# Head norm through selectors into one bank, and products of constants at the borders of stages

## The reference, cut to what matters

```python
h = rms_norm_2(h_res, norm_gain[li]);  proj = h @ w_in[li]
f_in, q, k, v, gate = jnp.split(proj, splits, axis=-1)
f_out = fourier_mixer(f_in, w_fourier[li])
q = q.reshape(b, l, N_ATTN_HEADS, 2, HEAD_DIM)        # 4 x 2 heads of 64
k = k.reshape(b, l, N_ATTN_HEADS, 2, HEAD_DIM)
q = apply_partial_rotary(rms_norm_2(q, q_norm_gain[li]), cos, sin)
k = apply_partial_rotary(rms_norm_2(k, k_norm_gain[li]), cos, sin)
...
o = diff_attention(q, k, v, lam)
y = jnp.concatenate([f_out, a_out], axis=-1) * jax.nn.silu(gate)
h_res = h_res + y @ w_out[li]
```

## Time and profile before

| | |
|---|---|
| median of 3 runs | 2792.8 us (2792.77 to 2797.52) |
| the profiled execution's own time | 2796.85 us |
| its span in the trace | 2795.1 us |
| PE busy | 2642.2 us, 95% of the span, 14429 matmuls |
| DVE, ACT, POOL busy | 1434.5, 1054.1 and 456.4 us |
| mean granted clock of the TensorE | 0.972 |

### The profile page before, as it was taken

One profiled execution on the slowest core, in us unless ns is written; L12 is line 12 of the kernel. 1 busy time (PEld: TensorE's weight loads), 2 busy tenths in 40 slices (PEclk: granted clock), 3 DMA queues, 4 the chain that ended last, 5 costly groups with the idle time before them and its releaser, 6 DMA issues. The chain is left out here.

```text
span 2795.1 us, 35915 instructions
## 1 busy us (share of the span) xinstructions
PE 2642.2 (95%) x14429; PEld 2265.9 (81%) x14429; DVE 1434.5 (51%) x2019; ACT 1054.1 (38%) x1846; POOL 456.4 (16%) x283
## 2 busy tenths in 40 slices
PE   5999869899889999999999999989999999989999
PEld 1877766899777888888888999779989999768987
DVE  5743682333457666666658423347743522326751
ACT  3412443444245334333344222157722222227740
POOL 0002201332000000000000000048820000008940
PEclk8999979999989999999999999999999999999999
DMA  5531101000211112112111233232122113233222
GB/s 234 181 132 48 41 5 53 16 1 1 106 39 53 38 61 61 44 48 61 46 53 48 92 82 82 78 78 47 43 101 106 48 42 84 57 106 74 55 83 84
DMA packets 67570, 189.46 MB, mean 68 GB/s; under 512 B 8016, under 2 KB 26832, under 8 KB 66512
## 3 DMA queue, kind: packets, MB, share of 16 engines
q1 hardware_dynamic: 67408, 187.22, 21.9%
HBM read 146.79 MB, written 16.97 MB: 59 GB/s over the span
## 5 line engine op out<-in xcount | busy, mean ns | idle before, releaser
L2649 DVE SCALAR_TENSOR_TENSOR res<-ps,gates,res 128x1024 f32<-128x1024 f32 x120 | 148.6, 1279 | 100.0 <-PE ps L2773 100.0
L1285 PE MATMUL ps<-h_hi,pf_wh 128*128 128x346 f32 (+2 forms) x800 | 187.8, 338 | 0.3
L1285 PE MATMUL ps<-h_lo,pf_wh 128*128 128x346 f32 (+2 forms) x800 | 183.0, 333 | 0.0
L2508 ACT ACTIVATE wo_wh<-ff_raw 128x512 fp32r<-128x512 f32 x120 | 75.3, 628 | 280.3 <-DVE ff_raw L2619 114.2
L1921 DVE TENSOR_REDUCE da_negmax<-ps 128x1 f32<-128x1040 f32 x136 | 167.9, 1236 | 20.9 <-PE ps L1775 14.1
L1906 POOL TENSOR_TENSOR da_E<-da_E,da_F 128x1040 f32<-128x1040 f32 x68 | 164.6, 2421 | 5.7
L2773 PE MATMUL ps<-ff_h_hi,wo_wh 128*128 128x512 f32 x512 | 157.8, 389 | 1.4 <-DVE res L2649 1.3
L1818 PE MATMUL ps<-da_aT,v 128*128 128x128 f32 (+1 forms) x1224 | 158.1, 275 | 0.7 <-ACT qk L1878 0.7
L2773 PE MATMUL ps<-ff_h_lo,wo_wh 128*128 128x512 f32 x512 | 157.7, 389 | 0.0
L2773 PE MATMUL ps<-ff_h_hi,wo_wl 128*128 128x512 f32 x512 | 157.6, 389 | 0.0
L1292 PE MATMUL ps<-h_hi,pf_wl 128*128 128x346 f32 (+2 forms) x800 | 152.4, 338 | 0.0
(11 more groups left out here) (540 smaller groups left out, 6154.9 us busy)
## 6 DMA issues: line engine op xcount, KB each, us to landing
ff_raw<-w_ff SPq DMA_DIRECT2D x48, 512.0 KB, 3.5
ada_w<-w_ada SPq DMA_DIRECT2D x16, 1024.0 KB, 7.3
ff_raw<-w_in SPq DMA_DIRECT2D x20, 512.0 KB, 4.1
pf_raw<-w_in SPq DMA_DIRECT2D x20, 512.0 KB, 4.2
wo_raw<-w_out SPq DMA_DIRECT2D x18, 512.0 KB, 4.4
residual_spill<-res SPq DMA_DIRECT2D x16, 520.0 KB, 3.1
st_q<-st_q_rounded SPq DMA_DIRECT2D x32, 260.0 KB, 5.1
ada_w<-w_ada SPq DMA_DIRECT2D x4, 2048.0 KB, 16.8
```

The lines of the kernel that those rows point to most:

```text
L1285: pe.matmul(bank(i * 2 + s, s)[c], wh[:, s, q * P:(q + 1) * P], x(q)[:, a:a + ln], start=(q == 0 and n == 0), stop=False)
L2508: act.activation(ring(wh, i), src, ACT.Copy).then_inc(s_hi, 1)
L2649: last = dve.scalar_tensor_tensor(out=res[:, m, :], in0=k.ps[:, b:b + 2, :].rearrange("p c w -> p (c w)"), scalar=gate[:, m:m + 1], in1=re ...
```

## The change

It has two parts. The diff below is cut to its core.

**Head norm.** ACT squares tile n and then rounds the square (hi, line `s_hi`); DVE makes the rest (lo, `rests`). A selector `pick` of 128 partitions and mostly zeros is the stationary operand: a window of 128 columns of it has two columns with ones, at row `32 c + 2 n` and the next of the output. Six matmuls per tile n (hi and lo, three chunks) add the sums of both half heads and of chunk c into rows `32 c + 2 n` of one bank, all 48 into the same 348 columns. They stand at (m, 7), and for the odd n at (m + 1, 3), one tile later than before. DVE multiplies the 128 x 348 sums twice by the root R (copied to the same layout), ACT takes one root with scale and epsilon per partition, DVE the reciprocal, a product by R, ACT rounds, DVE takes the rest. There are no transposes. Each of the 24 pieces has its own 128 x 128 selector, made by POOL.

**Products of constants.** `busy(n)` issues n matmuls of the constant `ones` with the identity, 128 x 128 in float32, into a bank that is not in use; nobody reads them. A stage gets some before its first work (`before`) and some after its last one (`behind`, after the wait that frees the bank).

```diff
+def busy(pe, k, bank, n):
+    for _ in range(n):
+        pe.matmul(k.ps[:, bank, 0:P], k.ones[:], k.ident[:], start=True, stop=True)
 ...
+                busy(pe, k, idle_bank, before)
                 loop(pe, body)
+                if behind:
+                    pe.wait_ge(freed[0], NI)
+                    busy(pe, k, 0, behind)
 ...
-    SUMS = {(m, 3 + 4 * i): 2 * m + i for m in range(4) for i in range(2)}
-    TURNS = {(4, 4): 0, (4, 5): 1, (4, 7): 2}
+    SUMS = {(m, 7): 2 * m for m in range(4)} | {(m + 1, 3): 2 * m + 1 for m in range(4)}
     SPREAD = {(5 + u // 8, u % 8): u for u in range(24)}
 ...
-            pe.wait_ge(self.s_sq, n + 1)
-            for t in range(self.NT):
-                w = min(P, L2 - t * P)
-                mm = pe.matmul(k.ps[0:w, 6, 16 * t + 2 * n:16 * t + 2 * n + 2], self.sq[n % 2][:, t * P:t * P + w],
-                               k.half_ones[:, 0:P:64], start=True, stop=True)
+            pe.wait_ge(self.s_lo, n + 1)
+            for i, sq in enumerate((self.hi[n % 2], self.lo[n % 2])):
+                for c, (a, w) in enumerate(self.cx):
+                    first = self.ones_at - self.row(n, c)
+                    mm = pe.matmul(k.ps[:, 6, 0:w], self.pick[:, first:first + P], sq[:, a:a + w],
+                                   start=(n == 0 and i == 0 and c == 0), stop=(n == self.N - 1 and i == 1 and c == len(self.cx) - 1))
             mm.then_inc(self.s_ssq, 1)
 ...
-            pe.matmul(k.ps[:, 6 + u % 2, 0:w], row, self.rh[:, a:a + w], start=True, stop=False)
-            pe.matmul(k.ps[:, 6 + u % 2, 0:w], row, self.rl[:, a:a + w], start=False, stop=True).then_inc(self.s_sp, 1)
+            pe.matmul(k.ps[:, 6 + u % 2, 0:w], self.spread[u][:], self.rh[:, 0:w], start=True, stop=False)
+            pe.matmul(k.ps[:, 6 + u % 2, 0:w], self.spread[u][:], self.rl[:, 0:w], start=False, stop=True).then_inc(self.s_sp, 1)
 ...
                 if n >= 2:
                     act.wait_ge(self.s_ssq, n - 1)
-                act.activation(self.sq[n % 2][:], self.qk[:, n, :], ACT.Square).then_inc(self.s_sq, 1)
+                act.activation(sq, self.qk[:, n, :], ACT.Square).then_inc(self.s_sq, 1)
+                act.wait_ge(self.s_sq, n + 1)
+                act.activation(hi[:], sq, ACT.Copy).then_inc(self.s_hi, 1)
 ...
+    def rests(self, dve, m):
+        for n in (2 * m, 2 * m + 1):
+            dve.wait_ge(self.s_hi, n + 1)
+            dve.tensor_tensor(self.lo[n % 2][:], self.sq[n % 2][:], self.hi[n % 2][:].bitcast(F32), ALU.subtract).then_inc(self.s_lo, 1)
 ...
         if m == 4:
             dve.wait_ge(self.s_ssq, self.N)
+            dve.tensor_tensor(self.rs[:], k.ps[:, 6, 0:self.w], self.root[:], ALU.mult).then_inc(self.s_var, 1)
+            dve.wait_ge(self.s_var, 1)
+            dve.tensor_tensor(self.rs[:], self.rs[:], self.root[:], ALU.mult).then_inc(self.s_var, 1)
             dve.wait_ge(self.s_sd, 1)
+            dve.reciprocal(self.rs[:], self.rs[:]).then_inc(self.s_r, 1)
+            dve.wait_ge(self.s_r, 1)
+            dve.tensor_tensor(self.rs[:], self.rs[:], self.root[:], ALU.mult).then_inc(self.s_r, 1)
+            dve.wait_ge(self.s_rh, 1)
+            dve.tensor_tensor(self.rl[:], self.rs[:], self.rh[:].bitcast(F32), ALU.subtract).then_inc(self.s_rl, 1)
```

More of the change, by code:

```diff
@@ L1406, in _ @@
             def _(pe):
+                busy(pe, k, 7, before)
                 for g, ts in enumerate(groups):
@@ L1429, in _ @@
                     pe.sem_inc(summed, 1)
+                if behind:
+                    pe.wait_ge(out_lo if split else out_hi, 5)
+                    busy(pe, k, 4, behind)
             if side:
@@ L1842, in _ @@
                         scores(g, 1)
+                    if i < 0:
+                        busy(pe, k, 7, 6)
                     if 0 <= i < NG:
@@ L2288, in latent_attention @@
     at0 = h0 + 4 * 5152 + MH * LT * 4
-    gemm(nc, k, "uk", rows(d["w_uk"]), MH, 2, lambda q: kh[:, q, :], lambda q: kl[:, q, :], call, preloaded=True, norm=norm, then=("mv", lambda q: d["w_mv"][q % 2 * P:(q % 2 + 1) * P, :], MH * MV, 3), side=keys,
+    gemm(nc, k, "uk", rows(d["w_uk"]), MH, 2, lambda q: kh[:, q, :], lambda q: kl[:, q, :], call, preloaded=True, norm=norm, before=14, behind=4, then=("mv", lambda q: d["w_mv"][q % 2 * P:(q % 2 + 1) * P, :], MH * MV, 3), side=keys,
          evac_act=copy_out(lambda m, a, w: kraw[:, m, a:a + w] if isinstance(m, int) else kraw[:, bass.ds(m, 1), a:a + w], call))
@@ L2292, in latent_attention @@
                 lambda q, a: kh[:, q, a:a + P], lambda q, a: kl[:, q, a:a + P],
-                list(range(0, LT, P)), lambda t: (v[:, t, :],), preloaded=True, then=("uq", rows(d["w_uq"]), 3 * P, 2))
+                list(range(0, LT, P)), lambda t: (v[:, t, :],), preloaded=True, behind=4, then=("uq", rows(d["w_uq"]), 3 * P, 2))
     qpe = k.sb("q_pe", [P, MH, L], k.res0 - 512)
@@ L3627, in project @@
             silu(act, m - 12, s, i, banks, freed, first)
-    gemm(nc, k, f"pf{li}", rows(d["w_in2"], R0), 20, KD, XH, XL, cx, evac_act=project, evac_dve=times_root, preloaded=True, norm=norm, late=norm,
+    gemm(nc, k, f"pf{li}", rows(d["w_in2"], R0), 20, KD, XH, XL, cx, evac_act=project, evac_dve=times_root, preloaded=True, norm=norm, late=norm, before=7, behind=6,
          split_first=k.split[f"pf{li}"], chunks_at=lambda m: cg if isinstance(m, int) and m >= 12 else cx,
@@ L3637, in second_layer @@
                 lambda q, a: hh[:, q * L2 + a:q * L2 + a + P], lambda q, a: hl[:, q * L2 + a:q * L2 + a + P],
-                list(range(0, L2, P)), lambda t: (v[:, t, :],), preloaded=True, side=stacks, row_scale=norm.rc, also=last_silu)
+                list(range(0, L2, P)), lambda t: (v[:, t, :],), preloaded=True, side=stacks, row_scale=norm.rc, also=last_silu, before=2, behind=8)
     yb = qk
@@ L3660, in second_layer @@
         own = [k.sb(f"pf1_first_{part}", [P, KD * P], p0 + 4096 * x, F32R)[:] for x, part in enumerate(("hi", "lo"))]
-        more = dict(follow=follow, then=("pf1", rows(d["w_in2"], 20 * P), KD * P, 2), split_next={1: own}, stored=follow.s_kept,
+        more = dict(follow=follow, behind=5, then=("pf1", rows(d["w_in2"], 20 * P), KD * P, 2), split_next={1: own}, stored=follow.s_kept,
                     store_tile=lambda m: (spill[:, m:m + 1, :], k.res[:, m:m + 1, :]) if isinstance(m, int)
@@ L3712, in project @@
         last.then_inc(freed, 1)
-    gemm(nc, k, "ina", rows(d["w_ina"]), 8, KD, XH, XL, cx, norm=n1, preloaded=True, split_first=tuple(per_slot(t) for t in k.split["ina"]), then=("inb", rows(d["w_inb"]), KD * P, 2),
+    gemm(nc, k, "ina", rows(d["w_ina"]), 8, KD, XH, XL, cx, norm=n1, before=12, behind=4, preloaded=True, split_first=tuple(per_slot(t) for t in k.split["ina"]), then=("inb", rows(d["w_inb"]), KD * P, 2),
          evac_act=project,
@@ L3743, in first_block @@
                                 gain=lambda q: k.a1[:, 2, q:q + 1], shift=lambda q: k.mod[:, 24 + q, 0:1])], y0, F0 + 72 * L)
-    mix_out(nc, k, d["xT"], "wo1", rows(d["w_out"]), yh, yl, cx, k.gates[:, 0, :], L, norm=split, first_raw=k.raw["wo1"], preloaded=True, follow=n2, then=("ff", rows(d["w_ff"]), KD * P, 2), split_next={})
+    mix_out(nc, k, d["xT"], "wo1", rows(d["w_out"]), yh, yl, cx, k.gates[:, 0, :], L, norm=split, first_raw=k.raw["wo1"], preloaded=True, follow=n2, before=12, then=("ff", rows(d["w_ff"]), KD * P, 2), split_next={})
     n2.keep_tiles(k.sb("ffn_in_kept", [P, 4, 4, L // 2], F0 + 40 * L), fh, fl)
```

134 lines of the change are left out of this document (66 added, 68 removed).

## The result

The kernel after the change takes 2746.55 us (median of 4 runs, 2744.62 to 2751.60) beside 2793.58 us before (4 runs): a ratio of 0.983 [0.9815, 0.9849]. The measured time lies 5.6 us above the forecast of 2741 us and inside its range; 47.0 us were won where 51.5 were forecast. Between the two profiled executions it is 50.6 us (2796.85 to 2746.22, where 2745.3 was forecast for the latter).

A forecast was written before the change was run, and what follows sets the result against it. PE was taken as the bound, busy 2642 of 2795 us. From the profiled 2796.85 us, 31.4 for the head norm and 20.1 net for the clock gave 2745.3; less 4.05 to the median, 2741 us, range 2722 to 2766.

The forecast's parts named there:

- Head norm, removed and added: In pf0 and pf1: 33.7 us of old work go per layer, 15.2 us of new work and 2.8 of waits come.
- The waits: PE waits in each head norm layer, mainly 0.5 us in gate 2 and 2.1 at the third spread; 2.8 us together.
- second rival: Head norm spreads keep 0.34 us per matmul despite 128 rows, 17.3 us dearer: 2758 us; chance 0.10.
- Clock, what is won back: At the 21 half-speed stretches, which lose at most 54.6 us: 16.6 and 6.0 us come back through the products.
- ten short stretches: Half-clock stretches after one border or in the attention's first steps: 20.7 us lost, 8 tenths or 16.6 us expected back.
- the five longer ones: Half-clock stretches at ina, uk, wo1, kept norm with feed-forward's start, and wo20: 17.9 us lost, a third or 6.0 expected back.
- The six unserved: Six half-clock stretches that get no product, 31.80 us of busy time: nothing expected back.
- The products' own cost: Products behind and ahead of stages overrunning their waits: 2.5 us in all, between 0 and 12.
- the prediction's own signs of being wrong: Clock at 0.975 or less, waits of 1 us and more on sq_lo at many sums, or new barrier waits for PE.
- The first rival: Clock not held at stage borders, stretches stay or move; 31.4 us less 3 us of cost: 2764 us; chance 0.20.
- the slower one: Head norm sums wait for a chain of three engines, over 3.2 us at each of 16; 2805 us at 4; chance 0.03.
- The last one: The change only shifts the low clock to dearer places; within the first rival's time, no chance of its own given.

The follow-up runs named there:

- norm alone: The changed kernel without its 211 products of constants, so the new head norm only; 2766.23 us, ratio 0.990 to the kernel before.
- the early sums: The changed kernel with the sums of odd tiles at (m + 1, 1) in place of (m + 1, 3); 2744.48 us, ratio 0.984.
- the kernel with 16 rows: The changed kernel with the head norm's spreads multiplying only the 16 rows that carry values, in place of 128; 2764.47 us, ratio 0.990.
- the one with transposes: The changed kernel with each product of constants replaced by two transposes of the same tile; 2747.99 us, ratio 0.984.
- the one with doubled products: The changed kernel with the 103 products ahead of stages doubled to 206; 2759.59 us, ratio 0.989.
- the fastest: The changed kernel with odd sums earlier, further products in unserved waits, and 128-row selectors in wo20 and wo21; 2733.82 us, ratio 0.979.

## Why the prediction was right, and where it was not

**Head norm, removed and added (31.4 us): right, and by its steps.** The norm alone took 15.35 us off `pf0` and 14.98 off `pf1`, 30.3 in all (27.7 by medians, 32.7 by spans). The new sums and spreads cost a gemm matmul's time, the end of the bounds that was taken. The waits are 2.4 us in `pf0` and 2.8 in `pf1` where 2.8 were worked out: 0.53 and 0.7, 0.17 and 0.33, 1.71 and 1.72, where the steps had 0.5, 0 to 0.3 and 2.1. The mechanism behind the last is shown by the early sums. POOL's selectors and SP's returning rows made no wait.

**The spreads' price (second rival): refuted** by the kernel with 16 rows, which is 17.9 us slower.

**Clock, what is won back (22.6 us of 54.6): mis-sized, too low.** All ten short stretches went, not 8 tenths: 20.7 us in place of 16.6. Of the five longer ones 35.9 us of busy time at the low clock became 14.1, and 10.4 of it are products: 3.7 us of other work in place of 35.9, so 16.1 us were won where a third, 6.0, was taken. The six unserved gave 1.0 (31.8 became 29.8), and the two new stretches took 3.2 (6.46 us of work). Together 34.6 us. The busy times say the same: with the norm alone PE is busy for 2607.0 us, with the products as well for 2629.8, 22.8 more, while the products themselves are busy for 58.9 us, as their group in the changed kernel shows. So all other work got 36.1 us faster.

```profile
L1057 PE MATMUL ps<-ident,ones 128*128 128x128 f32 x422 | 58.9, 295 | 16.6 <-PEq L66 16.2
```

**The products' own cost (2.5 us): the step that failed.** Of their 58.9 us, 40.8 lie in time in which PE was idle (155.4 with the norm alone, 114.6 with both). The other 18.1 us were lost again: idle time that did not shrink by as much as the products fill, or that grew elsewhere. The step costed ten or so borders at 0 to 0.3 us and called the waits a cover; its upper bound was 12. It asked only whether the products fit into the wait that they stand in, and reckoned with nothing for the other waits that grow when PE comes earlier. The net is 36.1 - 18.1 = 18.0 us where 20.1 were forecast. Two errors of some 14 and 16 us, of opposite sign, left an error of 2: that the net came out right is luck.

Products at the low clock take twice the time, but that is not where the 18.1 us went. Ahead of `ina`, PE waits for the norm even after its slow products:

```profile
64.33 0.71 PE L1273 MATMUL ps<-hn_hi,ina_wh 128*128 128x512 f32 x2 [0.83 <-DVE hn_lo L745]
```

The first matmul of `uk` starts 8.50 us after the last group of retention does, where it was 8.35 us before the change. And the latent attention starts 7.38 us after the last matmul of `uq`, as it did before: the 22 products there, at full clock, were free. Four kinds of places show where the time did go.
- Behind `pv` the cover was over too soon. The end of `pv0`, PE first, with its eight products:

```profile
1814.32 0.40 PE L1428 MATMUL ps<-pv_wl,h_hi 128*128 128x512 f32 x1
1814.87 2.02 PE L1057 MATMUL ps<-ident,ones 128*128 128x128 f32 x16
1817.65 0.72 PE L1785 MATMUL ps<-st_k,st_q 128*128 128x264 f32 x3 [0.76 <-PEq L66]
```

and ACT's evacuation of the last tiles:

```profile
1812.68 2.86 ACT L1372 ACTIVATE v<-ps,bn_root_turned 128x512 f32<-128x512 f32 x4 [5.58 <-PE ps L1428]
```

ACT is done at 1815.54, but the attention can't start before the products end, at 1816.89, and then 0.76 us later. They cost some 1.4 us in either layer. This is a wait of the barrier for the PE, one of the prediction's own signs of being wrong. The half clock at the start of `pv0` (3.4 us in the kernel before, 1.7 lost) is gone with the change, and yet `pv0` and `pv1` came out at -0.14 and +0.12 us.
- Work that comes earlier waits for something that doesn't. Waits of PE for weights inside `ina` and for the rotation in `inb`, before the change and then after it (total, times, longest, us):

```profile
PE ps L414 <- DVE rope_rs L431: 2.6, 1, 2.6
...
PE ps L1285 <- ACT ina_wh L1173: 0.7, 1, 0.7
```

```profile
PE ps L415 <- DVE rope_rs L432: 4.8, 1, 4.8
...
PE ps L1287 <- ACT ina_wh L1175: 3.1, 1, 3.1
```

`ina_wh` and `rope_rs` are not made earlier because PE is: 2.4 and 2.2 us more are waited for them (2.1 and 2.2 against the norm alone), and behind the first of these waits is the new stretch at 89.5. What `ina` gains at its start it loses in this wait, and the new stretch makes it 1.54 us longer.
- In the same way PE now waits 1.2 us for `uk_wh`, for which it waits neither before nor with the norm alone.
- In the two differential attentions the products are busy for 11.2 us, but PE idles only 6.3 us less than with the norm alone. The two stages together, with the norm alone and then after the change:

```profile
sum 385.62, PE 364.80; mean PE 182.40
```

```profile
sum 380.91, PE 366.42; mean PE 183.21
```

So 4.9 us of what the faster work freed there did not shorten the stages.

Of the 18.1 us these places hold about 2.8 + 4.3 + 1.2 + 4.9 = 13.2, the waits taken against the norm alone; the rest, some 5 us, is spread over the other borders and stays open.

**The tail of the attention.** The prediction weighed that transposes might not count, so that four products behind it could not repair `wo20`. In the changed kernel's trace `wo20` is 4.32 us shorter, nothing is left of the stretch at its start, and without the attention's products it is 4.35 us longer. But the repair isn't sure: of the ten profiled kernels that have these products, five have no low clock at the start of `wo20`, three have 3.3 us of it (the one with transposes, the one with doubled products, the fastest) and two have 10.2 us. In one of these two, without the products ahead of stages, `wo20` takes 115.11 us, as if it had none. One execution each doesn't say what decides it. That transposes count as activity is shown by the kernel with transposes alone.

**The first rival (clock not held, 0.20) and the slower one (0.03).** The first is decided by the clock, 0.972 with the norm alone and 0.988 with both. The slower one needed 3.2 us of wait at each of 16 sums; two of the sums wait, 0.53 and 0.7 us. The last one, that the clock only moves to dearer places, falls with the first: PE's busy time at the low clock went from 109.2 to 50.3 us.

## What to carry to other kernels

Where a small matmul is threaded among full ones, give it the rows of its neighbours, with zeros, before asking whether it can be smaller: here 16 rows cost 0.34 us more per pair than 128. The waits ahead of stages (3.1 to 7.4 us here) lose twice, in idle time and in half clock behind it. Products of constants can win the second part back if they fill the wait and no more. Half of what they won here (18 of 36 us) was lost again, in products that outlasted their cover and in waits that don't shrink. Look for the event that doesn't move (a DMA, a reduction) behind each border before counting its gain.

## What the runs showed of the hardware

- Float32 transposes of 128 x 128 keep the granted clock up as products do (0.986 to 0.990 in four executions, and 0.987 to 0.989).
- The same wait does not always cost the clock. PE waits 2.21 us for `wo_wh` in `wo20` before the change and after it. Before, the clock stays at 1.00 around it:

```profile
2086.00:2090.00 4.00, 2.38 (x15) 1.00 0.33 133
```

  After, the stretch at 2052.2 follows it at half clock. The products didn't bring this about: the kernel with the norm alone has the stretch too, at 2068.3. Of the eleven profiled kernels that leave this wait empty, the kernel before is the only one without it; the two that fill it don't have it. So a wait of this length is a risk, not a fixed price.
- The same kernel, the one without products behind stages, took 2748.3 us with a mean clock of 0.986 and 2760.0 with 0.982. Five runs of the fastest kernel lay within 3.3 us (2733.34 to 2736.64), but so did four of the kernel without products ahead (2759.05 to 2761.69), so a small spread is not a sign of filled waits.
- A float32 product of 128 columns takes 0.28 us of busy time on the average over the kernel (58.9 us for 211), not the 0.22 us worked out from the earlier trace rows, where eight records follow each other at full clock; part of that, about 5.2 us of the 12.5 in all, is the half clock (half of the 10.4 us above).
